# A fused two-block layer on one core: twelve projection blocks instead of eight beside the gated recurrence

## What is computed

```python
h = rms_norm(x, norm_w)
proj = h @ w_in                       # 1024 x 6160, split into
(gq, gk, gv, glr, hq, hf, hi, xq, gate) = split(proj)   # 512 512 1024 16 512 512 512 512 2048
gla_log_a = log_sigmoid(glr @ w_gate_up + b) / 16
gla_o  = recurrence(gq * 128**-0.5, gk, gv, gla_log_a)  # 4 heads, key 128, value 256
hgrn_log_f, hgrn_k = functions of hf and a lower bound  # "forget gates"
hgrn_o = recurrence(hq, hgrn_k, hi, hgrn_log_f)         # 4 heads, key 128, value 128
xo = cross attention of xq with a memory of 256 rows    # 4 heads
mixed = concat(rms_norm of gla_o, hgrn_o, xo) * silu(gate)
x = x + mixed @ w_out
```

## Time and profile before

| | us |
|---|---|
| median of three executions | 2732.37 (2731.23 to 2736.39) |
| the profiled execution | 2738.65 |
| its span in the profile | 2736.5 |
| stage 1 on PE | 66 to 453 |
| stage 2 on PE | 453 to 908 |
| PE busy, share of the span | 2511.2 (92%) |
| DVE busy, share of the span | 1167.7 (43%) |

### The profile page before, as it was taken

How to read it: one execution, slowest core, us unless ns; L and a number is a source line. 1 busy time by engine, 2 the same in 40 slices (tenths; PEclk the granted TensorE clock), 3 DMA queues, 4 the chain that set the end, 5 groups by cost and what they waited for, 6 DMA issues and landing times.

```text
span 2736.5 us, 43521 instructions
## 1 busy us (share of the span) xinstructions
PE 2511.2 (92%) x16392; PEld 2186.7 (80%) x16392; DVE 1167.7 (43%) x2259; ACT 911.6 (33%) x1646; POOL 885.5 (32%) x962
## 2 busy tenths in 40 slices
PE   6999998899888698989999999999999999898986
PEld 5777997777777587989999888889796777686786
DVE  3001233999998323140000042433335554576535
ACT  4223543444433333131122233333233434543311
POOL 2122125777777112122222223323233332131113
PEclk9999999999999899999999999999999999999998
DMA  4223342333322430222223233231312223545611
GB/s 187 105 77 136 119 167 101 116 112 112 109 97 78 185 136 31 88 103 92 92 92 108 77 116 112 76 108 66 120 59 89 96 96 147 186 163 196 211 47 62
DMA packets 150619, 305.76 MB, mean 112 GB/s; under 512 B 11457, under 2 KB 75585, under 8 KB 139217
## 3 DMA queue, kind: packets, MB, share of 16 engines
q1 hardware_dynamic: 86224, 215.77, 22.5%
q10 hardware_dynamic: 64256, 88.10, 9.0%
HBM read 204.22 MB, written 99.61 MB: 111 GB/s over the span
## 4 chain that ended last, share of the span: by engine, by line
PE 53%; issue 23%; DVE 14%; POOL 4%; ACT 2%; DMA 2%; POOLq 1%; ACTq 0%; SPq 0%; DVEq 0%
PE bank L383 8%; PE bank L385 8%; PE bank L384 8%; PE bank L394 6%; PE bank L395 6%; PE bank L396 6%; POOL w_lo L349 2%; PE bank L1819 2%; PE bank L1799 2%; DVE rec_z L1007 2%; DVE rec_z L1006 2%; PE bank L1240 1%; DVE rec_scores L1115 1%; PE bank L1788 1%; PE bank L622 1%
## 5 line engine op out<-in xcount | busy, mean ns | idle before, releaser
L394 PE MATMUL bank<-w_hi,at_hi 128*128 128x256 f32 x2432 | 705.4, 290 | 38.7 <-DVE at_lo L1422 29.0
L395 PE MATMUL bank<-w_lo,at_hi 128*128 128x256 f32 x2432 | 693.6, 285 | 0.0
L396 PE MATMUL bank<-w_hi,at_lo 128*128 128x256 f32 x2432 | 693.5, 285 | 0.0
L349 POOL TENSOR_TENSOR w_lo<-w_raw,w_hi 128x2048 fp32r<-128x2048 f32 x82 | 378.2, 4612 | 942.4 <-ACT w_hi L362 942.4
L383 PE MATMUL bank<-at_hi,w_hi 128*128 128x512 f32 x1472 | 617.4, 419 | 29.2 <-DVE at_lo L1422 12.3
L385 PE MATMUL bank<-at_hi,w_lo 128*128 128x512 f32 x1472 | 581.9, 395 | 0.0
L384 PE MATMUL bank<-at_lo,w_hi 128*128 128x512 f32 x1472 | 580.4, 394 | 0.0
L394 PEld LDWEIGHTS bank<-w_hi,at_hi 128*128 128x128 f32 x2432 | 471.5, 194 | 55.0 <-issue 36.8
L395 PEld LDWEIGHTS bank<-w_lo,at_hi 128*128 128x128 f32 x2432 | 472.8, 194 | 0.3
L396 PEld LDWEIGHTS bank<-w_hi,at_lo 128*128 128x128 f32 x2432 | 472.2, 194 | 0.0
L414 ACT ACTIVATE stage<-bank 128x512 f32<-128x512 f32 x272 | 162.0, 596 | 804.0 <-PE bank L385 445.4
(11 more groups left out here) (245 smaller groups left out, 3040.6 us busy)
## 6 DMA issues: line engine op xcount, KB each, us to landing
w_raw<-in_weights SPq DMA_DIRECT2D x84, 1024.0 KB, 6.0
feat<-stage ACTq DMA_DIRECT2D x152, 256.0 KB, 2.0
tok<-stage ACTq DMA_DIRECT2D x104, 256.0 KB, 2.2
stage<-feat SPq DMA_DIRECT2D x32, 256.0 KB, 3.3
x<-in_x SPq DMA_DIRECT2D x4, 1024.0 KB, 9.7
w_mem<-in_w_mem SPq DMA_DIRECT2D x4, 1024.0 KB, 11.6
logg<-gate_g ACTq DMA_DIRECT2D x8, 512.0 KB, 3.2
rec_b<-logg SPq DMA_DIRECT2D x16, 256.0 KB, 5.7
```

The source lines that it names most:

```text
L349: pool.tensor_tensor(w_lo[b][:], w_raw[:, b, :, :], w_hi[b][:].bitcast(F32), ALU.subtract).then_inc(w_split, 1)
L394: nc.tensor.matmul(o, ah, wh, start=(k == 0), stop=False)
L395: nc.tensor.matmul(o, ah, wl, start=False, stop=False)
L396: last = nc.tensor.matmul(o, al, wh, start=False, stop=(k == KT - 1))
```

## The change

- Stage 1 keeps 12 blocks: HF (2), Q1 (2), K1 (2), four of the six value blocks (form T), GATE (2). The two HQ blocks (F) and the two value blocks of the HGRN heads (T) move to stage 2.
- Stage 2 has 12 blocks beside 8 heads: three parts in a chunk instead of two (`REC_PARTS`), two ahead of the state's products and one behind the output's. Their order is gate (2), then in pairs of HQ and gate blocks (2, 2) around the value blocks (2), XQ (2), gate (2). SP's loads in `head_sp` get waits for the blocks that have to be stored first.
- In stage 2 `split_low` runs on DVE (`low_after`, at the end of a chunk) instead of on POOL: 12 of them, as against 8 on POOL (7 in heads 1 to 7 and one at the end).
- In `rec_products` the levels of the two halves alternate.
- In stage 1 the loads and operands of the first head (`first_sp`, `first_dve`, `first_pool`, `decays`) come ahead of the forget gates; `gate_logs` of the first pair is spread over the tiles of a block; the last two HGRN heads' `forget_logs` now come beside the two GATE blocks, each ahead of that block's `split_high`.

```diff
         gemm1 = [
             Segment(2, "F", ACT.Copy, feat1, HF),
             Segment(2, "F", ACT.Copy, feat1, Q1, P ** -0.5),
             Segment(2, "F", ACT.Copy, feat1, K1),
-            Segment(2, "F", ACT.Copy, feat1, HQ),
-            Segment(6, "T", ACT.Copy, tok1, 0),
+            Segment(4, "T", ACT.Copy, tok1, 0),
             Segment(2, "F", ACT.Copy, feat1, GATE),
         ]
         gemm_rec = [
-            Segment(6, "F", ACT.Copy, feat1, GATE + 2 * CB),
+            Segment(2, "F", ACT.Copy, feat1, GATE + 2 * CB),
+            Segment(2, "F", ACT.Copy, feat1, HQ, step=GATE + 4 * CB - HQ),
+            Segment(2, "T", ACT.Copy, tok1, 4 * CB),
+            Segment(2, "F", ACT.Copy, feat1, HQ + CB, step=GATE + 4 * CB - HQ),
             Segment(2, "F", ACT.Copy, feat1, XQ),
+            Segment(2, "F", ACT.Copy, feat1, GATE + 6 * CB),
         ]
...
+            first_pair = gemm1[3].first // 2 + 1
+            load_pair(sp, first_pair)
+            all_stored(sp, gemm1[:3])
             first_sp(sp)
-            gemm_sp(sp, gemm1[5:])
+            load_pair(sp, first_pair + 1)
+            gemm_sp(sp, gemm1[4:])
...
-            gemm_act(act, gemm1[2:3])
-            for step_ in range(3):
-                gate_logs(act, 0, step_)
-            gemm_act(act, gemm1[3:4])
+            s = gemm1[2]
+            for n in range(s.n):
+                for i in range(4):
+                    evacuate(act, s, 0, n, i)
+                    if n and i < 3:
+                        gate_logs(act, 0, i)
+                split_high(act, s, 0, n)
             gate_inputs(act, 1)
-            s = gemm1[4]
+            s = gemm1[3]
             for n in range(s.n):
                 for i in range(4):
                     evacuate(act, s, n // 2, n % 2, i)
                     if n == 0 and i < 3:
                         gate_logs(act, 1, i)
-                    if 1 <= n <= HEADS and i < 3:
-                        forget_logs(act, n - 1, i)
+                    if n == 1:
+                        decays(act, 0, gla, i // 2, i % 2)
+                    if n > 1 and i < 3:
+                        forget_logs(act, n - 2, i)
                 split_high(act, s, n // 2, n % 2)
-                if 1 <= n <= HEADS:
-                    forget_logs(act, n - 1, 3)
-            s = gemm1[5]
+                if n > 1:
+                    forget_logs(act, n - 2, 3)
+            s = gemm1[4]
             for n in range(s.n):
                 for i in range(4):
                     evacuate(act, s, 0, n, i)
-                    if i < 2:
-                        decays(act, 0, gla, n, i)
+                    if i < 3:
+                        forget_logs(act, HEADS - 2 + n, i)
+                forget_logs(act, HEADS - 2 + n, 3)
                 split_high(act, s, 0, n)
...
+        REC_PARTS = REC_BLOCKS * 4 * PARTS // (2 * HEADS * NT)
...
+        def rec_tiles_of(head, c):
+
+            n = (head * NT + c) * REC_PARTS
+            return range(n // PARTS, (n + REC_PARTS) // PARTS)
...
-                if head and c == 1:
-                    split_low(pool, (REC_AT + head + 1) // 2, (head + 1) % 2)
...
+        def low_after(dve, tile):
+
+            if tile % 4 == 3:
+                n = REC_AT + tile // 4 + 2
+                split_low(dve, n // 2, n % 2)
...
                 if then:
                     rec_place(dve, *then)
+                if head or c:
+                    for n in rec_tiles_of(head - (c == 0), (c - 1) % NT):
+                        low_after(dve, n)
...
+        def beside_results(act, head, c):
+
+            for n in rec_tiles_of(head, c):
+                evacuate(act, *rec_tile(n))
+                if n % 4 == 3:
+                    split_high(act, *rec_block(n // 4))
...
-                gemm_part(pe, *beside_head(head), c // 2, 2 * (c % 2))
+                beside_chunk(pe, head, c, range(REC_PARTS - 1))
...
-                gemm_part(pe, *beside_head(head), c // 2, 2 * (c % 2) + 1)
+                beside_chunk(pe, head, c, range(REC_PARTS - 1, REC_PARTS))
...
+            for j in range(1, LEVELS):
+                for b in range(2):
+                    rows = slice(b * BLK, (b + 1) * BLK)
+                    z = rZ[:, u, j, tok][:, rows]
+                    nc.tensor.matmul(to[rows, j - 1, :], z, z, start=True, stop=True)
             for b in range(2):
                 rows = slice(b * BLK, (b + 1) * BLK)
-                for j in range(1, LEVELS):
-                    z = rZ[:, u, j, tok][:, rows]
-                    nc.tensor.matmul(to[rows, j - 1, :], z, z, start=True, stop=True)
...
-            low_of(pool, gemm1[:5])
+            low_of(pool, gemm1[:3])
+            for b in range(2):
+                split_low(pool, gemm1[3].first // 2 + 1, b)
             first_pool(pool)
-            low_of(pool, gemm1[5:])
+            for b in range(2):
+                split_low(pool, gemm1[3].first // 2 + 2, b)
+            low_of(pool, gemm1[4:])
```

More of the change, by code:

```diff
@@ L415, in evacuate @@
             if s.form == "F":
-                row = it * (2 * CB) + (s.at0 + b * CB + (i // 2) * P)
+                row = it * (2 * CB) + (s.at0 + b * s.step + (i // 2) * P)
                 to = s.dest[bass.ds(row, P), (i % 2) * HALF:(i % 2 + 1) * HALF]
@@ L675, in p1_pe @@
                 last.then_inc(gl_prod, 1)
-            for n in (1, 3):
-                gemm_pe(pe, gemm1[max(n - 1, 1):n + 1])
-                low_rank_gates(pe, n - 1)
-                low_rank_gates(pe, n)
-            gemm_pe(pe, gemm1[4:])
+            for n in (1, 2):
+                gemm_pe(pe, gemm1[n:n + 1])
+                low_rank_gates(pe, 2 * n - 2)
+                low_rank_gates(pe, 2 * n - 1)
+            gemm_pe(pe, gemm1[3:])
         def low_rank_gates(pe, h):
@@ L808, in p1_dve @@
                                                    ALU.subtract).then_inc(g_dve, 1)
+            first_dve(dve)
             dve.wait_ge(gl_ld, 48)
@@ L831, in p1_dve @@
                 nc.vector.tensor_scalar(k, k, rest, None, ALU.mult).then_inc(g_dve, 1)
-            first_dve(dve)
         r_const, r_in_g = sem("r_const"), [sem("r_in_g0"), sem("r_in_g1")]
@@ L874, in build, with rec_block, rec_tile, beside_chunk @@
         REC_AT = gemm_rec[0].first
-        def beside_head(head):
-            s = gemm_rec[head // 6]
-            return s, head % 6 // 2, head % 2
+        REC_BLOCKS = sum(s.n for s in gemm_rec)
+        REC_PARTS = REC_BLOCKS * 4 * PARTS // (2 * HEADS * NT)
+        def rec_block(n):
+            return gemm_rec[n // 2], 0, n % 2
+        def rec_tile(n):
+            return *rec_block(n // 4), n % 4
+        def rec_tiles_of(head, c):
+            n = (head * NT + c) * REC_PARTS
+            return range(n // PARTS, (n + REC_PARTS) // PARTS)
+        def beside_chunk(pe, head, c, parts):
+            for n in parts:
+                part = (head * NT + c) * REC_PARTS + n
+                gemm_part(pe, *rec_tile(part // PARTS), part % PARTS)
         def half(h):
@@ L905, in load_gate, with block_stored, query_stored, value_stored @@
                          ).then_inc(r_in_g[h], 16)
+        def block_stored(sp, block):
+            for n in range(SLOTS):
+                sp.wait_ge(stored[n], 16 * (REC_AT + block + 2))
         def gate_stored(sp, head):
-            block = head if head < HEADS else HEADS + (head - HEADS) // 2
-            if block >= 2:
-                for n in range(SLOTS):
-                    sp.wait_ge(stored[n], 16 * (REC_AT + block - 2 + 2))
+            if 2 <= head < HEADS:
+                block_stored(sp, head - 2)
+            elif head >= HEADS:
+                block_stored(sp, 3 + 4 * ((head - HEADS) // 2))
+        def query_stored(sp, head):
+            if head >= HEADS:
+                block_stored(sp, 2 + 4 * ((head - HEADS) // 2))
+        def value_stored(sp, head):
+            if head >= HEADS:
+                block_stored(sp, 4 + (head - HEADS) // 2)
         def store_mixed(sp, head, mixer, h):
@@ L946, in p2_sp, with blocks_begun, block_of_head @@
             sp.wait_ge(r_st, 16 * (2 * 2 * HEADS + 1))
+        def blocks_begun(head, h):
+            n = (head * NT + CH * h) * REC_PARTS
+            per = 4 * PARTS
+            return range(-(-n // per), -(-(n + CH * REC_PARTS) // per))
+        def block_of_head(sp, head, h):
+            for n in blocks_begun(head, h):
+                load_block(sp, REC_AT + n + 2)
         def head_sp(sp, head, mixer, after):
-            load_block(sp, REC_AT + head + 2)
+            block_of_head(sp, head, 0)
             if after:
@@ L954, in head_sp @@
                 load_gates(sp, head + 1, 0)
+                query_stored(sp, head + 1)
                 sp.wait_ge(r_o, head * 8 + (3 + 8))
@@ L959, in head_sp @@
                 sp.wait_ge(r_o, head * 8 + (4 + 8))
+                value_stored(sp, head + 1)
                 load_values(sp, head + 1, after, 0)
@@ L962, in head_sp @@
             store_mixed(sp, head, mixer, 0)
```

(13 more changed lines are left out.)

13 lines of the change are left out of this document (6 added, 7 removed).

## The result

The changed kernel takes 2661.62 us (2660.84 to 2662.44, four executions) against 2734.38 (2731.23 to 2736.76) for the kernel before: a ratio of 0.9735, 95% interval 0.9718 to 0.9752. The forecast was 2654, its range 2638 to 2685. The profiled execution took 2662.27 and its span is 2660.5, 76.0 less than before.

The account below looks back on a forecast made before the run. PE's list was taken to bound stage 1 and DVE's the recurrence. Stage 1 -91.3, late split +3.5, heads +12 and the end -2.2 sum to -78 us: 2732.4 - 78 = 2654 us, range 2638 to 2685.

Parts of the forecast that it names:

- Stage 1, -91.3 forecast: Stage 1 loses four blocks (89.6 us) and PE's wait of 1.7 us, all on PE's list: -91.3 us.
- The late `split_high`, +3.5: End of stage 1: last forget step stands ahead of the last `split_high`, so DVE restarts 3.5 us later relative to PE.
- Alternation, 0.6 us a chunk: Stage 2 products: alternating halves run side by side, 1.60 us becomes about 1.0; GLA chunk 7.08 us.
- the costly rival: Alternation gains nothing, weight loads wait for the other half's passes; heads +37 instead of +12 us, total 2679; 15%.
- Splits on DVE, 2.5 us each: Stage 2 heads: each `split_low` on DVE takes 2.5 us, between bounds of 2.29 and 4.56.
- the seams: Stage 2: handing work between two nearly full engines, PE and DVE, costs 0.6 us for each of seven heads.
- the seams are worse: GLA chunks wait in turn for DVE and PE, half a us each: 32 us instead of 4, total 2682; 12%.
- Head 7, 48 forecast: Last head prepares no next one and follows PE: 7.3 chunks of 6.41 us, with waits 48 us against 44.7.
- The end, -2.2: Behind the last head the last split takes 2.3 us on DVE instead of 4.5 on POOL: -2.2 us.
- Slower than before: DVE stands at `low_after` for `split_high`, 6.5 us each time, eating the gain: 2732 us and more; 2%.
- The signs named ahead: Right: products 1.0 us, GLA heads 57 to 59.5, HGRN heads 54 to 56.5; wrong: heads over 61 us.
- the sum of -78: Whole kernel: -91.3 + 3.5 + 12 - 2.2 = -78 us, giving 2654 us (-2.9%).

Follow-up runs that it names:

- order, splits and both alone: Kernel before, no blocks moved, with only alternating products, 2722.12 us; only its eight `split_low` of the recurrence on DVE, 2716.79; both edits, 2714.37.
- the two with the step and the split exchanged: Changed kernel with `split_high` ahead of the last forget step, 2661.41 us; also with chunk 6 splits put off and each head's last turn moved, 2650.90.
- both edits undone: Changed kernel with the old order of products and the splits back on POOL, leaving the block move and new stage 1 order: 2697.72 us.

## Why the prediction was right, and where it was off

**Stage 1, -91.3 forecast, -96.5 between the two profiles.** The forecast was nearer than the profiles make it seem. In the three other profiles with the old stage 1 (order, splits and both alone) the first products come at 450.5, 449.2 and 450.5, not 453.45. In the nine with the new one they come between 356.98 and 360.7, at 358.75 in the mean. From the mean of the three, 450.1, that is 91.3 less; with the profile of before among the old ones it is 92.2. What the profile of before has above them is clock. Stage 1 has two places where PE makes eight small products for the decay logs (L688), which use 16 of its 128 rows. PE is never idle there, and half clock follows. The window of the first place, and PE's timeline in it:

```profile
160.00:190.00 30.00, 30.00 (x111) 22.28 (x110) 5.72 (x2) 6.42 (x7) 4.55 (x1) 0.89 0.20 71
```

```profile
168.28 4.15 PE L688 MATMUL bank<-glrT,w_up 16*128 16x512 f32 x8
...
172.95 0.63 PE L384 MATMUL bank<-at_lo,w_hi 128*128 128x512 f32 x1
173.38 0.63 PE L385 MATMUL bank<-at_hi,w_lo 128*128 128x512 f32 x1
```

Behind the small products the block's rows start 0.43 us apart instead of 0.23, and they do so until 178.4 in the profile of before, but only until 175.5 in that of both edits alone, where the same window is granted 0.94. The second place, 260 to 290, is granted 0.89 and 0.94 as well. 5 points of clock over 60 us are 3 us. In the profile of the changed kernel it is the other way round, 1.8 us below the mean of the nine; there PE's one wait in this stage, of 3.5 us in the stretch from 66 to 160, varies too (PE's idle time up to 354 is 3.1 to 5.0 us in the nine). One execution's stage 1 is good to about 3 us either way.

**The late `split_high`, +3.5: measured +3.7.** The chain was the one named: forget step, DVE's two instructions, two DMA issues, split at 361.48, POOL, DVE at 368.06. The eight other executions with the new stage 1 agree: 11.1 to 11.4 us, 9.0 in the two with the step and the split exchanged. The exchange takes off 2.1 and not 3.5 (above).

**Not in the sum: +2.5 from DVE's restart to the first output.** The forecast put this stretch at nothing. Here are its rows before (first fence) and after (second), of ACT and of PE:

```profile
465.42 1.06 ACT L1024 ACTIVATE rec_z<-rec_z 128x1024 f32<-128x1024 f32 x1 [9.31 <-DVE rec_z L1007]
...
467.09 0.48 PE L1247 MATMUL bank<-ident,rec_z 128*128 128x128 f32 x1 [9.61 <-ACT rec_kT L1184]
...
470.77 1.06 PE L1214 MATMUL bank<-rec_v,rec_scores 128*128 128x256 f32 x2
```

```profile
372.68 1.28 ACT L1081 ACT_TABLE_LOAD   x1 [9.29 <-DVE rec_z L1064]
...
375.65 0.47 PE L1320 MATMUL bank<-ident,rec_z 128*128 128x128 f32 x1 [15.91 <-ACT rec_kT L1255]
...
380.76 0.59 PE L1285 MATMUL bank<-rec_v,rec_scores 128*128 128x256 f32 x2
```

Two things have come in. First, ACT now loads a function table for 1.28 us ahead of its first exponential. Before, the last functions that ACT ran in stage 1 were the exponentials of `decays`, and no load stood there; in the new order they are those of a forget step. From DVE's restart to PE's transpose it is 375.65 - 368.06 = 7.59 us instead of 467.09 - 460.79 = 6.30, and all nine executions with the new stage 1 have this load, the four with the old one don't. Second, the first chunk has two parts of a block in front of its output instead of one: from the transpose to the output it is 5.11 us instead of 3.68. Together 2.7 by the rows' starts. The average clock of the stretch is lower than before (0.66 between 357 and 382, 0.73 between 453 and 472), but that is not the cause: in both kernels PE comes back from its wait at half clock (rows 0.43 us apart), and in the changed one it has the full clock back at 379.3, ahead of the output.

**Alternation, 0.6 us a chunk: measured 0.63** (1.60 to 0.97), and the chunk 7.03 against 7.08. The Trainium skill ("TensorE: Matmul & The Clock Gate", section "The mechanism") has a weight load overlap running matmuls only where the row groups differ. The halves share all rows and differ in columns. The measurement decides against the rule here: 28 passes, 14 of each half, take the time of 14, and the 24 weight loads of the levels lie within 0.78 us. Taken alone on the changed kernel the order is worth 16.1 us. Without it the heads come to 470.4 us in the windows of the earlier trace rows, where the costly rival gave 468.7, or 472.6 with its seams, and a GLA chunk to 7.69 where it gave 7.68. The rival of 15% is excluded, and its price was right.

**Splits on DVE, 2.5 us each: measured 2.36 in the mean**, most at 2.27 to 2.29, three at 2.56 to 2.62. The stalls of 4 us went with POOL's splits, and came back with them.

**The step that was off: the seams**, "I add 0.6 us for each of seven heads", 4.2 us in all. The first seven heads took 409.7 us against the 399.2 that the larger engine's time and these seams came to, so the term was 14.7 instead of 4.2. It is not 0.6 in each head: heads 1, 3 and 5 came at 57.2, 57.5 and 54.5, where 57.2, 59.1 and 53.8 were forecast. Heads 0, 2, 4 and 6 came 4.5, 3.1, 1.9 and 1.9 above. I had put the splits on the heads by number and not by place. One in chunk 6 delays the last `gated`; PE stands at the turn; the clock falls by half for some 7 us; DVE, which has just caught up, waits for PE. The run with these four splits moved shows the cause: 14 us gone from these heads, all in the step from one head to the next, and 400.2 left for the first seven. It does not part the wait from the half clock behind it. It also shows that this was no free gain, as DVE's load in heads 1, 3, 5 and 7 then counts and takes 6 back. The prediction held against this that `gated` has some 2 us of slack; no row shows this slack, and the earlier trace rows has PE waiting for `gated` 28 times. The rival "the seams are worse" had the right engines, but spread a loss of 32 us over all chunks; it is in four places, 11 us above the forecast.

**Head 7, 48 forecast, 44.5 measured.** It follows PE, as said, but its last chunk makes no products for a next one and takes 4.7 us, not the 6.41 counted for each, and PE waits in the head only once, for 0.5 us. This gives back 3.5 of the 10.5.

**The end, -2.2: measured -3.8.** The term itself is right: from the last output's row to the first products of the next stage it was 15.4 us and is 13.3, so -2.1, and it is 15.9 and 16.2 in the two kernels with the split back on POOL. The further 1.6 us lie in the later stages, whose code is the same and whose length differs by 6 us between the thirteen profiles.

**Slower than before** needed DVE to stand 6.5 us at each split. DVE stood for `split_high` once, for 1.9 us. In stage 1 nobody else came late.

**The signs named ahead** came out mixed. The products of 1.0 us, the twelve DVE rows of 2.3 to 2.6 and the missing 4 us stalls are there. But heads 0 and 2 took 61.7 and 62.4 us, which was named as a sign of being wrong, heads 4 and 6 took 58.2 where 54 to 56.5 was named, and PE is busy for over 97% only in heads 1 and 3 of the GLA heads. All of these are the seams again.

So the sum of -78 stands against -76.0 of the two profiles. It agrees in part by chance: +6 in the recurrence and +2.5 at the restart were made up by 5.2 in stage 1, all of them chance of these two executions (against the mean of the others stage 1 gives the forecast 91.3), and by 1.6 at the end. Against the medians of the same four-run comparison the gain is 72.8.

## What to carry to other kernels

When two engines are both nearly full and hand work to each other, place a long instruction by the chunk and not only by the head. By one execution, the same 2.3 us cost 3.6 us each ahead of a head's last handover (14.3 / 4), where PE's wait also takes its clock, and 1.4 us in the next head's first chunk (5.7 / 4). Work moved beside such a stage cost it less here than it took off elsewhere (34 us for 90, with PE busy for 87% ahead of it), and the edits that shorten each engine's list were worth more after the move (16.1 to 19.5) than before it (10.6 and 11.9), each by one execution. When the last function that ACT runs ahead of a stage changes, count the table load that the next one then needs on the path (1.28 us here). Streams of passes that use different columns of the array should alternate in the list (0.97 instead of 1.60 us for 28 passes).

## What the runs showed of the hardware that I had not expected

PE's granted clock is only loosely tied to how full PE is. By the windows of the recurrence:

| kernel | PE busy | granted clock |
|---|---|---|
| order alone, no blocks moved | 84% | 0.95 |
| both edits, no blocks moved | 87% | 0.92 |
| before | 89% | 0.97 |
| splits on DVE alone, no blocks moved | 91% | 0.97 |
| changed, splits on POOL | 92% | 0.96 |
| changed, both edits undone | 95% | 0.98 |
| changed | 95% | 0.97 |
| changed, splits of chunk 6 put off (first execution) | 95% | 0.99 |
| changed, splits of chunk 6 put off (five rounds) | 95% | 1.00 |
| changed, old order of products | 98% | 1.00 |

It is no strict order, and a half clock itself makes PE busier. What the traces show more firmly is what stood ahead of a dip: two waits of PE close together (1.69 and 1.64 us ahead of 0.51 for 7 us), or eight products on 16 of the 128 rows, in a stretch in which PE is never idle (then 3 to 6 us at half clock, 0.89 in one execution and 0.94 in another at the same place of the same code). So a part of what an edit takes from PE's list can be lost again at half clock; how much of the 22.5 - 15.9 us that the two edits without the move fell short is this, and how much DVE's list, was not separated.
